# Moving the modulation rows and the result products within the steps of a two-way chunked scan, and loading the weight pieces of both slots in turns

## The reference, cut to what matters

```python
mod = jax.nn.silu(c) @ ada_w[l] + ada_b[l]          # 6 rows of 1024: sh1, sc1, g1, sh2, sc2, g2
...
def step(S, inp):
    r_t, w_t, kk_t, b_t, v_t, k_t = inp
    sa = jnp.einsum("bhvk,bhk->bhv", S, kk_t)
    S = (S * w_t[:, :, None, :] - sa[..., None] * b_t[:, :, None, :]
         + v_t[..., None] * k_t[:, :, None, :])
    return S, jnp.einsum("bhvk,bhk->bhv", S, r_t)
...
S, ys = lax.scan(step, state0, xs, reverse=reverse)  # for both directions d = 0, 1; y = sum of both
```

## Time and profile before

| | |
|---|---|
| median of three runs | 1567.88 us (1564.88 to 1568.94) |
| profiled execution, its own time | 1571.56 us |
| profiled execution, span | 1570.0 us |
| TensorE busy | 1489.1 us of the span |
| VectorE busy | 920.6 us |
| ScalarE busy | 597.5 us |
| GpSimd busy | 272.7 us |
| mean granted TensorE clock | 0.962 |
| steps -1 to 10 | about 244 to 527 us of the span |

### The profile page before, as it was taken

The page is one execution under the profiler, slowest core; times in us unless marked ns, Lnnn a source line. Parts: engine busy times, 40 slices in busy tenths (PEclk is TensorE's granted clock), DMA queues, the critical chain, the costliest instruction groups (busy, mean ns, idle before and its releaser), DMA issues.

```text
span 1570.0 us, 35522 instructions
## 1 busy us (share of the span) xinstructions
PE 1489.1 (95%) x14858; PEld 1227.3 (78%) x14858; DVE 920.6 (59%) x1499; ACT 597.5 (38%) x1037; POOL 272.7 (17%) x290
## 2 busy tenths in 40 slices
PE   5999988999999989999999998998989999999997
PEld 3788865788899777887777887877878888888885
DVE  4424245588667748888886224767565655555222
ACT  4422344435342534444443223546664222322221
POOL 0000023565352010111111121000021111111110
PEclk9999997789879999999999999999999999999999
DMA  9232201233220222232223222221112232232221
GB/s 372 96 109 81 81 0 50 63 95 103 81 64 4 83 81 81 81 107 82 105 87 104 92 92 81 98 72 55 59 50 87 102 107 91 96 107 92 93 92 72
DMA packets 38987, 139.15 MB, mean 89 GB/s; under 512 B 3152, under 2 KB 3664, under 8 KB 38480
## 3 DMA queue, kind: packets, MB, share of 16 engines
q1 hardware_dynamic: 38720, 135.24, 25.4%
q10 hardware_dynamic: 144, 2.10, 0.3%
HBM read 135.22 MB, written 2.10 MB: 87 GB/s over the span
## 4 chain that ended last, share of the span: by engine, by line
PE 79%; DVE 13%; ACT 3%; issue 3%; DMA 1%; ACTq 0%; DVEq 0%; SPq 0%
PE bank L722 56%; PE bank L904 9%; DVE ffn_sb L3159 5%; PE bank L731 2%; PE bank L668 2%; PE bank L998 1%; DVE w_up L2587 1%; PE bank L1070 1%; PE bank L1010 1%; DMA arena<-w 1%; PE bank L935 1%; PE bank L661 1%; ACT w_up L1681 1%; ACT arena L2177 1%; DVE w_in L2587 1%
## 5 line engine op out<-in xcount | busy, mean ns | idle before, releaser
L722 PE MATMUL bank<-hf_hi,w_up 128*128 128x512 f32 x1376 | 424.0, 389 | 0.0
L722 PEld LDWEIGHTS bank<-hf_hi,w_up 128*128 128x128 f32 x1376 | 258.3, 188 | 53.2
L722 PE MATMUL bank<-hf_lo,w_up 128*128 128x512 f32 x688 | 269.1, 391 | 4.6 <-DVE w_up L2587 4.6
L722 PE MATMUL bank<-act_hi,w_down 128*128 128x512 f32 x704 | 216.7, 389 | 0.0
L904 PEld LDWEIGHTS bank<-arena 64*64 64x64 f32 x4224 | 161.1, 154 | 31.6 <-issue 19.3
L904 PE MATMUL bank<-arena 64*64 64x32 f32 (+1 forms) x4224 | 172.4, 237 | 7.8 <-DVE arena L2814 2.5
L1681 ACT ACTIVATE w_up<-ring 128x1024 fp32r<-128x1024 f32 x87 | 91.9, 1058 | 215.7 <-PE bank L722 215.7
L2587 DVE TENSOR_TENSOR w_up<-ring,w_up 128x1024 fp32r<-128x1024 f32 x87 | 106.8, 1229 | 97.0 <-ACT w_up L1681 97.0
L722 PEld LDWEIGHTS bank<-hf_lo,w_up 128*128 128x128 f32 x688 | 129.1, 188 | 36.1 <-DVE w_up L2587 8.8
L3159 DVE SCALAR_TENSOR_TENSOR ffn_sb<-ffn_sb 128x512 f32<-128x512 f32 x176 | 151.5, 861 | 5.4
L722 PEld LDWEIGHTS bank<-act_hi,w_down 128*128 128x128 f32 x704 | 132.1, 188 | 27.3
(11 more groups left out here) (350 smaller groups left out, 2388.8 us busy)
## 6 DMA issues: line engine op xcount, KB each, us to landing
ring<-w SPq DMA_DIRECT2D x76, 1024.0 KB, 4.8
ring<-w SPq DMA_DIRECT2D x32, 704.0 KB, 4.0
ring<-w SPq DMA_DIRECT2D x64, 256.0 KB, 3.0
arena<-w SPq DMA_DIRECT2D x8, 1024.0 KB, 18.2
x<-xT SPq DMA_DIRECT2D x1, 2048.0 KB, 10.2
x<-xT ACTq DMA_DIRECT2D x1, 2048.0 KB, 8.4
outT<-x SPq DMA_DIRECT2D x4, 512.0 KB, 2.7
arena<-ctxT SPq DMA_DIRECT2D x1, 1024.0 KB, 18.4
```

Of the source, the lines that this page charges most:

```text
L722: ins = mm(out, w[:, a, k, :], of_block(b, k0 + k), start=first and k == 0 and m == 0, stop=last and k == n - 1 and m == 2)
```

## The change

The change moves work and leaves out none.

- Step -1: both `ada_part` are issued behind `nx` of level 2. Before, they stood behind `nx` and behind `dx` of level 3.
- Steps 0 and 1: both stand behind `nx(m, 1, 2)`. Before, the first stood one product earlier and the second behind `state_terms(n, 1)`.
- Steps 2 to 6: the first moves from behind `results(n, 1)` to behind `nx(m, 0, 5)`, the second from there to behind `dx(m, 0, 5)`; `ada_select` moves from behind `nx(m, 0, 6)` to behind `dx(m, 0, 6)`.
- Steps 7 to 10 have a loop of their own: `results(n, 0)` moves from ahead of `nx(m, 0, 4)` to behind `nx(m, 0, 5)`, and `results(n, 1)` from behind `dx(m, 0, 4)` to behind `nx(m, 0, 6)`. VectorE's `second_result(n, 0)` moves from behind `x_turned(m, 0, 4)` to behind `x_out(m, 1, 5)`.
- ScalarE: `first_result(n, 1)` moves ahead of `ada_row_out(n)`.
- SyncE: `pace` is gone. The parts of both slots are issued in turns, slot 0, slot 1, slot 0 and so on; a slot's first part waits until the slot is free, each further one until the part ahead of it in the same slot has landed.

GpSimd's program stays as it is.

```diff
-            def pace(m, u, e):
-
-                if m < NCC - 2:
-                    return m, 2 * (3 + 2 * u) + e
-                return (m, 2 * 5 + e) if u == 0 else (m + 1, 2 * 2 + e)
-
-            def load_paced(g, at, m, u):
-
-                sp.wait_ge(s["product"], DONE[g - 2])
-                to = ring[:, g % 2, :].rearrange("p (c n) -> p c n", c=2)
+            def load_paced(m):
+
                 for e in range(PARTS):
-                    step, l = pace(m, u, e)
-                    sp.wait_ge(s[("nx_mm0", "dx_mm0")[l % 2]], 5 * step + l // 2 - 1)
                     c, half = e // 2, slice(KB * P // 2 * (e % 2), KB * P // 2 * (e % 2 + 1))
-                    sp.dma_start(to[:, c, half], w8[2 * at + c][:, half]).then_inc(s[f"slot_in{g % 2}"], 16)
+                    for u in range(2):
+                        g = PACED[2 * m + u]
+                        at = 21 + g - SLOT["ADA2"]
+                        to = ring[:, g % 2, :].rearrange("p (c n) -> p c n", c=2)
+                        if e == 0:
+                            sp.wait_ge(s["product"], DONE[g - 2])
+                        else:
+                            sp.wait_ge(s[f"slot_in{g % 2}"], 16 * (LANDED[g] - PARTS + e))
+                        sp.dma_start(to[:, c, half], w8[2 * at + c][:, half]).then_inc(s[f"slot_in{g % 2}"], 16)
...
@@ TensorE, step -1
             nx(m, 0, 2)
             nx(m, 1, 2)
+            ada_part(n, 0)
+            ada_part(n, 1)
             token_gate(1, 0)
             token_gate(1, 1)
             dx(m, 0, 2)
...
             nx(m, 0, 3)
             nx(m, 1, 3)
-            ada_part(n, 0)
             token_gate(3, 0)
             token_gate(3, 1)
             dx(m, 0, 3)
             dx(m, 1, 3)
-            ada_part(n, 1)
             token_gate(4, 0)
...
@@ TensorE, steps 0 and 1
+                nx(m, 1, 2)
                 ada_part(n, 0)
-                nx(m, 1, 2)
+                ada_part(n, 1)
                 dx(m, 0, 2)
                 updates(n, 1)
...
                 state_terms(n, 1)
-                ada_part(n, 1)
                 dx(m, 1, 3)
...
@@ TensorE, steps 2 to 6
-            for n in range(NCC - 2, NC - 1):
+            for n in range(NCC - 2, 7):
...
                 nx(m, 1, 4)
                 dx(m, 0, 4)
                 results(n, 1)
-                ada_part(n, 0)
                 dx(m, 1, 4)
                 nx(m, 0, 5)
+                ada_part(n, 0)
+                nx(m, 1, 5)
+                dx(m, 0, 5)
                 ada_part(n, 1)
+                dx(m, 1, 5)
+                nx(m, 0, 6)
+                nx(m, 1, 6)
+                dx(m, 0, 6)
+                ada_select(n)
+                dx(m, 1, 6)
@@ TensorE, steps 7 to 10
+            for n in range(7, NC - 1):
+                m, q = n + 1, n + 2
+                nx(m, 0, 2)
+                updates(n, 0)
+                nx(m, 1, 2)
+                scores(q, 0)
+                dx(m, 0, 2)
+                dx(m, 1, 2)
+                state_terms(n, 0)
...
+                updates(n, 1)
+                nx(m, 1, 3)
+                nx(m, 0, 3)
+                scores(q, 1)
+                dx(m, 1, 3)
+                turned(m, 0)
+                dx(m, 0, 3)
+                state_terms(n, 1)
...
+                nx(m, 0, 4)
+                turned(m, 1)
+                nx(m, 1, 4)
+                dx(m, 0, 4)
+                dx(m, 1, 4)
+                nx(m, 0, 5)
+                results(n, 0)
                 nx(m, 1, 5)
                 dx(m, 0, 5)
                 dx(m, 1, 5)
                 nx(m, 0, 6)
-                ada_select(n)
+                results(n, 1)
                 nx(m, 1, 6)
                 dx(m, 0, 6)
                 dx(m, 1, 6)
@@ ScalarE
                 tok_out(m, 0)
+                first_result(n, 1)
                 ada_row_out(n)
                 state_padded(m, 1)
-                first_result(n, 1)
                 state_padded(m, 0)
@@ VectorE, steps 7 to 10 (a loop of their own, as on TensorE)
-                second_result(n, 0)
                 x_out(m, 1, 4)
...
                 x_out(m, 1, 5)
+                second_result(n, 0)
                 w_out(m, 0, 6)
```

## The result

Over 20 runs of each the changed kernel has a median of 1570.19 us (1563.40 to 1582.54), the kernel before 1561.67 us (1552.35 to 1569.63). The ratio is 1.0055, with a 95% interval of 1.0035 to 1.0075. I had forecast 1562 us from a baseline of 1567.9 us, 6.1 us faster; it is 8.5 us slower. The time itself is inside my range, the direction is wrong.

A forecast was written before the change was run, and what follows sets the result against it. TensorE was taken as the bound, busy but slowed by stretches at 1.2 GHz. Terms -4 - 3.7 - 5 + 6.6 = -6.1 us, loads 0, gave 1562 us from a median of 1567.9 us; range 1547 to 1574 us.

The forecast's parts named there:

- The bound: Steps -1 to 10: TensorE is busy throughout but slow at 1.2 GHz, each us there costing about 0.44 us.
- otherwise indifferent: Within a step, order does not matter to a busy TensorE; gain must come from the clock, cost from a wait.
- Step -1: Pair of `ada_part` behind `nx` of level 2 lifts the clock some 14 us sooner: gain 4 us.
- Steps 0 and 1: Step 1's pair ends near 305 us instead of 312.4, 8.4 us less at 1.2 GHz: gain 3.7 us.
- Steps 2 to 6 (gain 5): Ends of these steps: shorter bare run of small products saves a third of 15 us, 5 us.
- Steps 7 to 10 (loss 6.6): `scores` waits twice 2.8 us for GpSimd's keys, low clock costs 7.0, a removed low stretch saves 6.0: loss 6.6 us.
- the credit of 6.0 us: Seam of steps 7 and 8: `results` break the bare run, removing 13.7 us at 1.2 GHz, worth 6.0 us.
- The loads (0): New order of weight-part loads: parts land in time for the next `ada_part`, so no cost, 0 us.
- The waits for GpSimd decide: Rival: late `results(n, 1)` stops TensorE at `scores`, low clock after; price 11.6 us, 1572 us, slower; chance 0.2.
- only gaps drop the clock: Rival: ends of steps 2 to 6 fall as before, waits cost 6.6 us; 1567 us, no measurable change; chance 0.17.
- everything thin is filled: Rival: clock stays up from step 2, GpSimd in time, 1539 us; with half the gain 1552 us; chance 0.18 together.
- The weight parts: Rival: weight parts land late, 1 to 3 us in a step; 1564 us and more; chance 0.05.

The follow-up runs named there:

- the front alone with the old loads: Kernel before with only both `ada_part` of steps -1 to 1 paired behind the second product of level 2, old loads: 1555.05 us, ratio 0.9951.
- the tails: Kernel before with only `ada_part` and `ada_select` of steps 2 to 6 moved, old loads: 1561.87 us, ratio 1.0019.
- the keys first: Changed kernel with GpSimd making erase rows and keys ahead of the decayed rows of the results: 1556.09 us, ratio 0.9975.
- the other kernel with the keys first: Kernel before with early `ada_part` pairs in steps -1 to 1, moved results and GpSimd's keys first, old loads; steps 2 to 6 as before: 1557.73 us, ratio 0.9974.
- the cover back: Changed kernel with results in their old places and `ada_part(n, 0)` of steps 2 and 3 ahead of `dx(m, 1, 4)` again: 1564.29 us, ratio 1.0028.
- the first experiment: Kernel before, unchanged, run again for a second profile and each run's time and mean clock: 1560.62 us, ratio 0.999.

## Why the prediction was wrong

**The bound** was read rightly: between steps -1 and 10 the clock and the waits of TensorE decide. That order within a step is "otherwise indifferent" is refuted. I had looked for waits on GpSimd only; at level 4 of steps 2 and 3 VectorE's `w_out` runs some 1.2 us late, and at the late `results` of steps 8 to 10 0.4 to 0.7 us. Waits for line 2798 (2766 before) come to 5.6 us in all against 1.8, 3.8 us that no term of mine held.

**Step -1** was right: the clock rose at 249.1 us, with the pair (246.2 to 249.5 us), and `state_terms` of step 0 comes after 33.2 instead of 38.2 us; 5.0 for 4. That the pair lifts it early holds in all nine profiles that have it. **Steps 0 and 1** gave 2.1 of 3.7 us: the clock rose with the pair there too, at 300.3 us, and fell once more from 314.0 to 324.2 us, longer than the 6.8 us before. My term held an error besides: it set the end of the new pair (305 us) against the rise of the clock (313.3 us); end against end (312.4 us) is 7.4 us, worth 3.3. Both together I had at 7.7; the front alone with the old loads measured 6.5 us. The mechanism holds.

**Steps 2 to 6 (gain 5).** In the profiles they give 6.6 us. Over many runs the tails give nothing, alone (ratio 1.0019) or on top of the front (0.9954 after 0.9951). The step that failed is the baseline: the sum is made "on the profiled execution's 1571.6 us", and its low stretches are taken for those of every execution. That time is above the highest of twenty (1569.63 us), its mean clock of 0.962 below the median of 0.967, and 0.005 at 1.15 us per 0.001 is 5.8 us of low clock that the median execution does not have and no edit can take away. The 34.2 us at 1.2 GHz, worth 15 us, were 10.2 us in the second profile, worth 4.5. Three runs at 1567.9 us agreed with the first; twenty say 1561.7.

**Steps 7 to 10 (loss 6.6)** is where the sign was lost, and the term of the sum that failed is the credit of 6.0 us for a seam that falls no more. The rest of the sum was near. The waits were 3.37 and 2.81 us, 6.2 for 5.6. The low stretches were 10.2 us each, TensorE busy in 10.2 and 8.2 us of them; at 0.44 that is 4.5 and 3.6, 8.1 for 7.0. Without the credit this is 14.3 us; undoing the part gave 15.1 by the medians and 12.2 by the ratios, the part alone cost 11.8 and 13.4. In the two profiled executions the credit is there, 14.3 - 6.0 = 8.3 against the stage's 8.7. In others it mostly is not. With the results in their old places the seam has 13.7 us at 1.2 GHz in two of ten profiles, both of before, 6.8 us in five and nothing in three, some 6.1 in the mean and so 2.7 us of credit. Nor do the new places keep the clock up: with the keys first and no wait the seam has nothing once and 13.7 us once, and the time was no lower (ratio 0.9975 against 0.9977). So the step that failed here is of the same kind as in steps 2 to 6: 11.0 us of gain, 5 and 6.0, were read from the low stretches of one slow execution. Between the two profiled executions the four stages come to -5.0 us, near my -6.1; over twenty runs of each kernel it is +8.5.

GpSimd took 5.27 us for the six operations at the first seam, beside two running sums on VectorE, and 4.71 us at the second, where there are none: 0.56 us more at one wait, where I had worked out 0.3 us at each. By the Trainium skill, page SBUF — State Buffer, section SBUF: two separate sides, the two engines exclude each other on a shared port; the trace agrees in that GpSimd is slower beside the sums, by 0.56 us for sums of 1.74 us. That either engine was shut out for a whole instruction of the other it does not show.

**The loads (0)** landed in 2.6 to 4.9 us, 3.1 in the median (2.4 to 4.3, 3.0), and no `ada_part` waited, as I said. Yet alone they cost 5.8 us (8.9 by the ratio), and beside the early pairs 1.0 to 5.3 us by one measure or the other. By what is not settled. The gap in step 1 is 0.9 us longer with the new loads in the mean of the profiles; what TensorE waits for in it the profile does not show, and whether it is late instructions was not tested.

**The rivals.** "The waits for GpSimd decide", at 1572 us and 0.2, is what happened, for the reason that it gave: waits with low clock, and ends of steps 2 to 6 that give nothing. That "only gaps drop the clock" is half true. At the waits of 3 us it fell in all four cases (here and with the results alone), with the same thin products ahead and the keys first in one of four. But at the seam of steps 8 and 9 it fell when TensorE had stood still for only 0.8 us (here) and 1.1 us (results alone). Shorter waits go either way: none of 1.2 us in steps 2 to 6 (108.2 us at 1.00 with 8.0 us idle) and none of the three of 1.6 us with the keys first is followed by a fall, both of 1.3 us with the cover back are. And the falls at 412.3 us and in the other kernel with the keys first have no such gap ahead of them. The Trainium skill, page TensorE: Matmul & The Clock Gate, section Why this matters for your kernels, blames idle gaps: the trace agrees at the seam of steps 7 and 8, where the clock fell 3.7 us after TensorE had stopped, and not at 412.3 us. Of "everything thin is filled" the clock came true, 1.00 from 324.2 us to the first wait, and "GpSimd is somehow in time" did not. The weight parts made no `ada_part` wait.

**The parts, one put on after another** (front, tails, loads, results), are -6.5, -1.0, +1.0 and +15.1 us by the medians, -7.6, +0.5, +3.6 and +12.2 us by the ratios: either way the front is gained, the results lose 1.6 to 2.3 times what it gives, and no other part is shown to gain.

## What to carry to other kernels

Before moving a producer later, walk through the queue of every engine that waits for it: here one GpSimd operation that nobody needed soon stood ahead of the keys that TensorE needed next, and putting the keys first was worth 12 to 14 us. A wait can cost more than its own length: here 3.1 us each in the mean, and 3.6 to 4.5 us more by the clock that fell with it. Take the low stretches of one profile as a draw: hold its mean clock and time against many runs before a gain is counted on them, and ask of each dense piece that you move which VectorE work it was hiding.

## What was not expected of the hardware

Time follows the mean granted clock from one execution of the same kernel to the next: by a straight line through each kernel's own runs 1.04 to 1.31 us less for each 0.001 more in all twelve experiments, over spreads of 0.006 to 0.019 in clock. The places of some low stretches change with it, as the two profiles of before show. A higher median clock is no gain by itself: the changed kernel had 0.971 against 0.967 (before, in the first experiment) and was 8.5 us slower.
